# Two attention sections: turned probabilities as the stationary operand, the sum's inverse applied to the result

## The reference, cut to what matters

```python
s = jnp.einsum('bhgnqd,bhgnkd->bhgnqk', qb, kb) * ATT_HEAD_DIM ** -0.5 + bias[None, :, None]
s = jnp.where(valid, s, NEG)
...
w = jax.nn.softmax(jnp.stack(lses, axis=0), axis=0)
o = (w[..., None] * jnp.stack(outs, axis=0)).sum(0)
```

```python
m = jnp.maximum(jnp.max(s, axis=-1, keepdims=True), sink_l)
p = jnp.exp(s - m)
denom = jnp.sum(p, axis=-1, keepdims=True) + jnp.exp(sink_l - m)
return jnp.einsum("bgrqk,bkgd->bqgrd", (p / denom).astype(vb.dtype), vb)
```

## Time and profile before

| | |
|---|---|
| median of 3 runs | 2461.74 us (2461.03 to 2464.47) |
| the profiled execution | 2464.69 us |
| its span, first to last instruction | 2462.9 us |
| PE busy | 2141.0 us, 87% of the span |
| PE weight loads busy | 2006.1 us |
| DVE busy | 1603.1 us |
| ACT busy | 1016.6 us |
| granted TensorE clock, mean | 0.926 |

### The profile page before, as it was taken

How to read it: one execution, slowest core, us unless ns; L and a number is a source line. 1 busy time by engine, 2 the same in 40 slices (tenths; PEclk the granted TensorE clock), 3 DMA queues, 4 the chain that set the end, 5 groups by cost and what they waited for, 6 DMA issues and landing times. The chain is left out here.

```text
span 2462.9 us, 37607 instructions
## 1 busy us (share of the span) xinstructions
PE 2141.0 (87%) x15762; PEld 2006.1 (81%) x15762; DVE 1603.1 (65%) x2753; ACT 1016.6 (41%) x1425; POOL 20.0 (1%) x36
## 2 busy tenths in 40 slices
PE   2889999879978999998799668988899779797997
PEld 1888888879978888898799667667899777687996
DVE  5767667567657676765654367964666488765664
ACT  1344454334433444443444233443544334444443
POOL 0000000000000000000000000000000000000000
PEclk6899999989988999999899878989999789898998
DMA  5345534447632454244465143211455132123551
GB/s 228 126 171 188 189 120 155 157 146 281 237 128 100 183 199 178 104 170 154 143 218 188 48 155 120 91 64 69 166 184 189 69 114 102 59 86 119 178 184 69
DMA packets 52366, 358.92 MB, mean 146 GB/s; under 512 B 5939, under 2 KB 8499, under 8 KB 9572
## 3 DMA queue, kind: packets, MB, share of 16 engines
q1 hardware_dynamic: 52196, 356.51, 40.1%
HBM read 355.40 MB, written 1.08 MB: 145 GB/s over the span
## 5 line engine op out<-in xcount | busy, mean ns | idle before, releaser
L344 DVE TENSOR_TENSOR w_lo<-raw,w_hi 128x1024 fp32r<-128x1024 f32 x340 | 410.9, 1227 | 294.6 <-ACT w_hi L609 292.8
L399 PE MATMUL projected<-u_hi,w_hi 128*128 128x256 f32 x1728 | 504.8, 292 | 87.2 <-DVE w_lo L344 49.2
L609 ACT ACTIVATE w_hi<-raw 128x1024 fp32r<-128x1024 f32 x340 | 352.0, 1054 | 390.4 <-PE projected L399 335.9
L399 PE MATMUL projected<-u_lo,w_hi 128*128 128x256 f32 x1728 | 498.8, 289 | 0.0
L399 PE MATMUL projected<-u_hi,w_lo 128*128 128x256 f32 x1728 | 497.9, 288 | 0.0
L399 PEld LDWEIGHTS projected<-u_hi,w_hi 128*128 128x128 f32 x1728 | 341.8, 198 | 95.7 <-issue 42.0
L1344 PE MATMUL projected<-u_hi,w_hi 128*128 128x256 f32 x1184 | 347.7, 294 | 46.3 <-DVE w_lo L1280 46.3
L1280 DVE TENSOR_TENSOR w_lo<-raw,w_hi 128x1024 fp32r<-128x1024 f32 x228 | 274.2, 1222 | 153.9 <-ACT w_hi L1534 153.3
L1344 PE MATMUL projected<-u_lo,w_hi 128*128 128x256 f32 x1184 | 343.9, 290 | 0.0
L1344 PE MATMUL projected<-u_hi,w_lo 128*128 128x256 f32 x1184 | 343.3, 290 | 0.0
L399 PEld LDWEIGHTS projected<-u_lo,w_hi 128*128 128x128 f32 x1728 | 341.7, 198 | 0.2
(11 more groups left out here) (343 smaller groups left out, 4055.6 us busy)
## 6 DMA issues: line engine op xcount, KB each, us to landing
raw<-in_stream_dram SPq DMA_DIRECT2D x324, 1024.0 KB, 4.9
w_mod<-in_first_ada_dram SPq DMA_DIRECT2D x8, 1024.0 KB, 14.1
band<-bias_rows SPq DMA_DIRECT2D x1, 3072.0 KB, 14.4
x<-in_xT_dram SPq DMA_DIRECT2D x1, 1024.0 KB
out_dram<-f_sq SPq DMA_DIRECT2D x2, 512.0 KB, 2.6
tri<-in_tri_dram SPq DMA_DIRECT2D x2, 384.0 KB, 4.6
c<-in_c_dram SPq DMA_DIRECT2D x1, 512.0 KB
mask<-in_mask_dram SPq DMA_DIRECT2D x1, 384.0 KB
```

The source lines that it names most:

```text
L344: eng.tensor_tensor(part(w_lo, step, half), raw_half(step, half), part(w_hi, step, half).bitcast(F32), ALU.subtract).then_inc(s_lo_pool if ...
L399: m = pe.matmul(out, a, b, start=start and n == 0, stop=stop and n == 2, **kw)
L609: act.activation(part(w_hi, step, half), raw_half(step, half), ACT.Copy).then_inc(s_hi, 1)
```

## The change

- The multiplication of the 128x512 probabilities is gone. PE turns `S` as ACT left it (it waits for `s_ae`, the exponentials, instead of `s_an`).
- In the values product the operands change places: a turned 128x128 piece of `PT` is stationary and 64 columns of `vA` stream. The output has the queries on the partitions and a head's 64 features in columns.
- DVE multiplies this output, 128x64 in the first network and 128x128 in the second, by the inverse from PSUM into `O` (two buffers, on the storage of `rstd` and `lnv`).
- When both units of a pair are in `O`, PE turns it back, in a new function `attention_output`: one 128x128 piece in the first network, two in the second. ACT rounds that to `o_hi` and DVE subtracts to `o_lo`, as before. This is step n + 4 (`OUTPUT`) for odd n, so both lists have one attention step more, which also moves where `interleave` puts the steps between the projections.
- The order inside a step: on PE the turning back comes first, ahead of the scores; on ACT and DVE the rounding and the subtraction of the pair come first; DVE's multiplication of `O` comes last. Each values product now also waits for `s_oe`, the multiplication of the unit before it.

```diff
-          "att": 2 * SLOTS + VALUES, "wa": 4, "wb": 2, "wo": 4, "ln": 2, "w1": FP, "w3": FP, "w2": FP}
+          "att": 2 * SLOTS + OUTPUT, "wa": 4, "wb": 2, "wo": 4, "ln": 2, "w1": FP, "w3": FP, "w2": FP}
...
             def attention_turn(l, n):
                 U = 2 * SLOTS * l + n
-                pe.wait_ge(s_an, U + 1)
+                pe.wait_ge(s_ae, U + 1)
...
                 pe.wait_ge(s_pt, U + 1)
+                if U:
+                    pe.wait_ge(s_oe, U)
                 if odd == 0 and U:
                     pe.wait_ge(s_o, U // 2)
-                out = MB[3][AD * odd:AD * odd + AD, j * P:(j + 1) * P]
+                out = MB[3][:, odd * AD:(odd + 1) * AD]
...
-                    m = pe.matmul(out, vA[:, s, f:f + AD], PT[:, b * P:(b + 1) * P], start=b == 0, stop=b == 3)
+                    m = pe.matmul(out, PT[:, b * P:(b + 1) * P], vA[:, s, f:f + AD], start=b == 0, stop=b == 3)
                 m.then_inc(s_av, 1)
+
+            def attention_output(l, n):
+                M = SLOTS * l + n // 2
+                pe.wait_ge(s_oe, 2 * M + 2)
+                if M:
+                    pe.wait_ge(s_o, M)
+                pe.transpose(MB[3][:, T:T + P], O[n // 2 % 2][:, 0:P], ident[:]).then_inc(s_ot, 1)
...
+                    if i >= OUTPUT and i % 2:
+                        attention_output(l, i - OUTPUT)
                     if i < 2 * SLOTS:
                         attention_scores(l, i)
-                    if i >= VALUES:
+                    if VALUES <= i < 2 * SLOTS + VALUES:
                         attention_values(l, i - VALUES)
...
-                        link(dve.reciprocal(rden[:, b:b + 1], den[:, b:b + 1]))
-                        dve.tensor_scalar(S[:, b, :], S[:, b, :], rden[:, b:b + 1], None, ALU.mult)\
-                           .then_inc(s_an, 1)
+                        dve.reciprocal(rden[:, b:b + 1], den[:, b:b + 1]).then_inc(s_rd, 1)
                     n = i - VALUES
-                    if n > 0 and n % 2:
...
+                    if 0 <= n < 2 * SLOTS:
+                        U, M = 2 * SLOTS * l + n, SLOTS * l + n // 2
+                        dve.wait_ge(s_av, U + 1)
+                        dve.wait_ge(s_rd, U + 1)
+                        if M >= 2:
+                            dve.wait_ge(s_ot, M - 1)
+                        dve.tensor_scalar(O[n // 2 % 2][:, n % 2 * AD:(n % 2 + 1) * AD], MB[3][:, n % 2 * AD:(n % 2 + 1) * AD],
+                                          rden[:, n % ABUF:n % ABUF + 1], None, ALU.mult).then_inc(s_oe, 1)
...
-WO_AFTER = (3, 5, 7, 9, 11, 13, 16, SH + VALUES - 1)
+WO_AFTER = (3, 5, 7, 9, 11, 13, 16, SH + OUTPUT - 1)
```

```diff
+                for a in range(2):
+                    m = pe.transpose(MB[3][:, T + a * P:T + (a + 1) * P], O[n // 2 % 2][:, a].rearrange("p o d -> p (o d)"),
+                                     ident[:])
+                m.then_inc(s_ot, 1)
```

More of the change, by code:

```diff
@@ L53 @@
 KB = 1024
-TURN, VALUES = 2, 3
+TURN, VALUES, OUTPUT = 2, 3, 4
 ABUF = 3
@@ L100, in plan_first @@
     ml += [("ml_mean", 0), ("ml_var", 0)]
-    att = [("att", i) for i in range(2 * SLOTS + VALUES)]
+    att = [("att", i) for i in range(2 * SLOTS + OUTPUT)]
     late = [("o", i) for i in range(4)] + [("gbr", i) for i in range(8)]
@@ L693, in _ @@
                     b = i % ABUF
+                    n = i - OUTPUT
+                    if n > 0 and n % 2:
+                        pair, j = n // 4, n // 2 % 2
+                        act.wait_ge(s_ot, SLOTS * l + n // 2 + 1)
+                        dst = o_hi[:, pair, :].rearrange("p (a j b) -> p j a b", j=2, b=2)[:, j]
+                        act.activation(dst, MB[3][:, T:T + P].rearrange("p (a b) -> p a b", b=2),
+                                       ACT.Copy).then_inc(s_oh, 1)
                     if TURN <= i < 2 * SLOTS + TURN:
@@ L918, in _ @@
                 elif kind == "att":
+                    n = i - OUTPUT
+                    if n > 0 and n % 2:
+                        pair, j = n // 4, n // 2 % 2
+                        dve.wait_ge(s_oh, SLOTS * l + n // 2 + 1)
+                        hi, lo = (o[:, pair, :].rearrange("p (a j b) -> p j a b", j=2, b=2)[:, j] for o in (o_hi, o_lo))
+                        dve.tensor_tensor(lo, MB[3][:, T:T + P].rearrange("p (a b) -> p a b", b=2),
+                                          hi.bitcast(F32), ALU.subtract).then_inc(s_o, 1)
                     if i < 2 * SLOTS:
@@ L1060, in plan_second @@
     plan += [("ssd_gate", 0), ("att2", 0), ("att2", 1), ("ssd_norm", 0)]
-    for i in range(2, SH + VALUES):
+    for i in range(2, SH + OUTPUT):
         plan += [("att2", i)]
@@ L1616, in _ @@
                     b = i % ABUF
+                    n = i - OUTPUT
+                    if n > 0 and n % 2:
+                        kv, j, _ = unit(n)
+                        act.wait_ge(s_ot, SH // 2 * l + n // 2 + 1)
+                        act.activation(o_hi[:, 2 * kv:2 * kv + 2, j * P:(j + 1) * P][:, :, ::-1],
+                                       halves(MB[3][:, T:2 * T]), ACT.Copy).then_inc(s_oh, 1)
                     if TURN <= i < SH + TURN:
@@ L1803, in _ @@
                 elif kind == "att2":
+                    n = i - OUTPUT
+                    if n > 0 and n % 2:
+                        kv, j, _ = unit(n)
+                        dve.wait_ge(s_oh, KT * l + n // 2 + 1)
+                        hi, lo = (o[:, 2 * kv:2 * kv + 2, j * P:(j + 1) * P][:, :, ::-1] for o in (o_hi, o_lo))
+                        dve.tensor_tensor(lo, halves(MB[3][:, T:2 * T]), hi.bitcast(F32), ALU.subtract).then_inc(s_o, 1)
                     if i < SH:
@@ L1822, in _ @@
                         link(dve.tensor_tensor(den[:, b, :], den[:, b, :], es[:, b, :], ALU.add))
-                        link(dve.reciprocal(den[:, b, :], den[:, b, :]))
-                        for odd in range(2):
-                            ins = dve.tensor_scalar(S[:, b, odd, :], S[:, b, odd, :], den[:, b, odd:odd + 1], None, ALU.mult)
-                        ins.then_inc(s_an, 1)
+                        dve.reciprocal(rden[:, b, :], den[:, b, :]).then_inc(s_rd, 1)
                     n = i - VALUES
-                    if n > 0 and n % 2:
-                        kv, j, _ = unit(n)
-                        dve.wait_ge(s_oh, KT * l + n // 2 + 1)
-                        hi, lo = (o[:, 2 * kv:2 * kv + 2, j * P:(j + 1) * P][:, :, ::-1] for o in (o_hi, o_lo))
-                        dve.tensor_tensor(lo, halves(MB[3][:, 0:2 * P]), hi.bitcast(F32), ALU.subtract).then_inc(s_o, 1)
+                    if 0 <= n < SH:
+                        U, M = SH * l + n, SH // 2 * l + n // 2
+                        dve.wait_ge(s_av, U + 1)
+                        dve.wait_ge(s_rd, U + 1)
+                        if M >= 2:
+                            dve.wait_ge(s_ot, M - 1)
+                        dve.tensor_tensor(O[n // 2 % 2][:, :, n % 2, :], MB[3][:, n % 2 * P:(n % 2 + 1) * P].rearrange("p (a d) -> p a d", a=2),
+                                          rden[:, n % ABUF, :].rearrange("p (a o) -> p a o", o=1).to_broadcast([P, 2, 64]),
+                                          ALU.mult).then_inc(s_oe, 1)
                 elif kind == "wo2" and i == 7:
```

51 lines of the change are left out of this document (26 added, 25 removed).

## The result

The changed kernel takes 2492.61 us (median of 4 runs, 2491.37 to 2492.78), the kernel before 2462.05 on the same chip: ratio 1.0122, 95% interval 1.0104 to 1.0139. It is 1.2% slower; 2488 was forecast. The profiled execution has a span of 2490.8 us, 27.9 more than before.

The account below looks back on a forecast made before the run. PE was taken as the bound (busy 131.2 of 137 us in the first network's attention). New waits of 13.1 us in the second network and 13.4 in the first, 26.5 together, on 2461.7 gave 2488 us, range 2474 to 2510.

Parts of the forecast that it names:

- the prediction's own signs of being wrong: Eight values passes taking 0.6 us, the four-microsecond wait missing, or PEclk falling in the second network's pairs.
- The load sets the pace: Values product: passes stay at about 0.11 us despite half the streaming columns, so 0 saved.
- the second rival: Values product runs by its streaming columns, at half the time: -28 us, 2460 to 2470; chance 0.07.
- (a): First network, step 2: the 1.9 us wait for `S` and 1.5 us of slow projection go, -3.4 us a layer.
- (b): First network, step 4, now together with step 3, waits for `O` behind `ada` work on DVE: +0.3 us a layer.
- (c): First network, step 5 behind `o` 3: wait for `o_lo` of 2.8 us in place of 2.25, +0.55 a layer.
- (d): First network, steps 6 and 7 behind `gbr` 0: 4.3 us idle, 0.15 for `o_lo`, 1.5 slow stretch, +5.95 a layer.
- (e): First network, steps 8 and 9: like a second-network pair, from a start without wait, +1.2 us a layer.
- (f): First network, steps 11, 13 and 15: hand-off chain behind a projection, partly covered by scores, 0.3 us each, +0.9 a layer.
- (g): First network, steps 16 to 19: two waits for `PT` (1.4 us) become waits for the chain (1.8), +0.4 a layer.
- (h): First network: the 0.2 us rest of the wait for `o_lo` falls, the turnings back add 1.0 us a layer.
- the rival of the clock: Second network's pairs and ends fall into slow stretches, 1.5 us each, 21 in all: 2509 us; chance 0.15.

Follow-up runs that it names:

- storage_only: The kernel before plus one small unused tensor (128x6) in the second network where the change allocates its second inverses, no instruction changed: 2452.99 us, ratio 0.996.

## Why the prediction was right, and where not

The sign and the size were right (2488 forecast, 2492.6 measured, within the range), and so was the mechanism: chains that PE waits for. But that the number is so close is luck. Two errors of opposite sign stand behind it: against storage_only, the partner with the same storage, the edits cost 39.6 us where the sum has 26.5, and storage gave 8.7 back. And of the prediction's own signs of being wrong one came: PEclk fell in the second network's pairs. The sum against the rows, in us of the profiled spans:

| | forecast | measured |
|---|---|---|
| first network, layer 1 and 2 | 6.7, 6.7 | 6.9, 7.0 |
| second network, layer 1 and 2 | 6.55, 6.55 | 7.1, 15.1 |
| outside attention | 0 | -8.3 |
| sum | 26.5 | 27.9 |

**Removed work.** The first turning's waits fell, as forecast, and DVE has 18 us less work (20 forecast; the multiplication of `S` took 35 us where 31 were taken). That this relief is nothing where it isn't waited for is not borne out: 45 us of load at the end of the steps cost 12.7. The multiplication of `O` took 0.27 where 0.2 was taken, and 0.29 as taken.

**The product.** "The load sets the pace": right, loads of 192 ns and eight passes in 1.10 us. But "about 0.11" a pass was read too low for the old product: to the next instruction's start its eight passes took 1.02 us, 0.128 each, and the new ones take 0.94, 0.118 each. So a small gain of 0.08 us a unit was there, 5 us in 64 units, where 0 was taken. The section "Back-to-back issue gap" of the Trainium skill's page "TensorE: Matmul & The Clock Gate" has the gap of a single product follow its streaming columns, which gave the second rival; it also says that in a stream of loads and products both set the spacing. The trace agrees with the second sentence: half the streaming with a longer load brought 8%, not half.

**First network.** (a) The 1.9 us wait is gone, and the turning and the projection behind it are 1.5 us shorter (before, 323.37 to 331.19 with the projection at 7.06; now 0.41 and 5.92): 3.4, as forecast. (b) 0.23 (0.3 forecast). (c) 2.78 in place of 2.25, as forecast to 0.02. (d) The wait: 4.04 against 4.3. Its slow stretch was too cheap: 1.5 was forecast for a projection alone, but scores, values, turning and most of `gbr` 1 ran slowly: from 358.66 to the next scores at 371.37 are 12.7 us, where turning back 0.20, scores 1.07, values 0.94, turning 0.54 and the projection's 5.84 of undisturbed places make 8.6; 4.1 for 1.65. (e) 0.46 + 0.35 = 0.8 against 1.2. (f) 0.39 each against 0.3. (g) 0.29 + 0.79 + 0.63 = 1.7 against 1.8. (h) A turning back takes 0.20, not 0.13, to the next instruction's start: 1.6 us a layer; the values gave back 16 times 0.08. Added up, the terms as read come to some 7.9; the stretch grew by 6.9. The rows have more than the difference: six projections with a turning back or a values product behind them take 5.83 us to its start, where every undisturbed one before took 5.93, and a turning of `S` is followed 0.04 to 0.05 us sooner, 16 times.

**Second network, a pair.** The wait for `O` was forecast at 1.05 and came as 0.99. The values start 5.18 us into the pair (forecast 5.35), 0.74 later than in storage_only; they and the turning behind them give 0.12 back. So the pair is 0.62 us longer than its partner with the same storage, where the sum said 0.95: right mechanism, the size half again too high.

**The step that failed** is in the rival of the clock: "One idle of 1.07 us left the clock at 1.00, so I count none." Nine of twelve pairs were followed by 1.2 GHz, eight of them at some 1.6 us inside the pair, and so were the ends: some 12 us in the pairs and, by estimate, some 16 with the ends. (By their granted clocks, 0.91 before and 0.88 and 0.82 now, the two stretches hold 9 and 26 us more at the lower level; at 0.21 us a pass in place of 0.11 about half of that is lost.) Only this explains that the fourth stretch grew by 8 us more than the third. That one place had stood a wait of this length was no evidence for a place with other work around it. It was given 0.15 as a case of its own, 1.5 us at each of 14 places; it happened at nine pairs and the ends, and its 2509 less the 8.7 of storage is 2500.

**What was not seen** is the storage: the diff showed `rden2`, 24 bytes, and nothing in the prediction asked what lies behind it. It gave back 8.7 us, 8.3 of the profiled span outside attention and 3.3 and 1.9 inside it; what the profiled executions show beyond 8.7 lies within what single runs differ.

**Shown and not shown.** Shown by experiment: that the second network's loss sits in the order and in the shared bank together (36 us come back without touching the product or the number of turnings), while the other bank alone and the other order alone bring nothing clear; that the storage's gain is independent of attention; that DVE's time matters by its place. Not shown: why three pairs of the first layer with the same 0.99 us wait stayed at full clock. The instructions and the idle time are the same, and an edit in the first network changed which pairs were hit. In the first network the other list alone brought 5.8 us in the two stretches, list and bank together 26; the bank alone did not run there.

## What to carry to other kernels

When an edit moves a scaling behind a product, follow the result all the way to the next writer of its bank: here the result had two waits behind it, one for the scaling and one for the shared bank, and taking away one of them brought 2 us of 36. Price a new wait with the slow clock that may follow it, and widen the range for it: here the idle time of a pair grew from 0.65 to 1.08 us, and the clock added 1.6 us in eight of twelve pairs. Compare against a copy of the old kernel with the new allocations, since a tensor of 24 bytes moved the time here by 8.7 us, a fifth of what the edits cost.

## What the runs showed of the hardware

- A float32 pass of 256 columns at full clock follows the one before at 0.113 to 0.120 us. Where its tiles lie in storage is part of it: moving an area by 64 bytes, with no instruction changed, made 48 of them take 5.46 us in place of 5.70, and the whole kernel 8.7 us faster. What else sets the pace is open.
- A wait of 0.96 to 0.99 us before two small products left the clock at 1.00 in three pairs and was followed by 1.2 GHz in nine. The wait of 0.65 us in the pairs of the kernel before was followed by it in none.
- Eight float32 passes with 128 stationary and 64 streaming columns take 0.94 us to the next instruction's start; with 64 stationary and 128 streaming 1.02. Twice the load (192 ns in place of 137) and half the streaming together are worth 8%.
